# Twelve of the gathered value rows added before the second expert stage, in one streaming-encoder step

## What is computed

```python
e = (jnp.take_along_axis(i1, j // PEER_TOPK, axis=-1) * N_KEYS
     + jnp.take_along_axis(i2, j % PEER_TOPK, axis=-1))
gate = jax.nn.softmax(top_s, axis=-1).astype(xt.dtype)
u = jnp.take(u_experts, e, axis=0)
v = jnp.take(v_experts, e, axis=0)
act = jax.nn.gelu(jnp.einsum('td,thkd->thk', xt, u), approximate=False)
return jnp.einsum('thk,thkd->td', gate * act, v)
```

## Time and profile before

| | |
|---|---|
| timed runs | 1658.46 us median, 1656.03 to 1667.42, 3 runs |
| profiled execution | 1659.93 us, of which its span 1657.1 |
| mean granted TensorE clock | 0.969 of full speed |
| busy, share of the span | TensorE 93%, VectorE 77%, GpSimd 50%, ScalarE 39% |
| DMA, mean over the span | 246 GB/s |

### The profile page before, as it was taken

One profiled execution on the slowest core, in us unless ns is written; L12 is line 12 of the kernel. 1 busy time (PEld: TensorE's weight loads), 2 busy tenths in 40 slices (PEclk: granted clock), 3 DMA queues, 4 the chain that ended last, 5 costly groups with the idle time before them and its releaser, 6 DMA issues.

```text
span 1657.1 us, 26947 instructions
## 1 busy us (share of the span) xinstructions
PE 1540.6 (93%) x9360; PEld 1505.7 (91%) x9360; DVE 1281.3 (77%) x2590; ACT 649.2 (39%) x838; POOL 831.5 (50%) x497
## 2 busy tenths in 40 slices
PE   6995188999999998999999998999999999999996
PEld 6995088999899998999999998999999999999996
DVE  7999998468899998678777741377777777777775
ACT  5332053333333333566665642433333333333332
POOL 5797043333666765666666676234444443344301
PEclk9998589999999999999999999999999999999998
DMA  4221021222766776799999999588998999999851
GB/s 172 90 76 51 0 80 39 90 76 86 245 224 224 267 246 217 284 361 368 359 359 361 348 386 392 184 313 328 344 341 328 356 336 327 329 343 342 327 187 54
DMA packets 149502, 407.59 MB, mean 246 GB/s; under 512 B 12224, under 2 KB 75968, under 8 KB 147648
## 3 DMA queue, kind: packets, MB, share of 16 engines
q1 hardware_dynamic: 89776, 215.27, 38.0%
q0 software_dynamic: 36864, 134.23, 21.6%
q10 hardware_dynamic: 22800, 57.42, 8.9%
HBM read 349.99 MB, written 56.89 MB: 246 GB/s over the span
## 4 chain that ended last, share of the span: by engine, by line
PE 74%; DMA 5%; DVE 1%; ACT 1%; POOL 0%; issue 0%; DVEq 0%; ACTq 0%
PE ps_unit L752 30%; PE ps_unit L812 18%; PE ps_misc L812 17%; PE ps_unit L568 5%; DMA acts_dram<-act_ring 3%; PE ps_misc L786 2%; DMA raw<-stream 1%; PE ps_misc L712 1%; ACT gates L1063 1%; DMA rows<-u_rows,expert 0%; DVE y_all L1623 0%; POOL w_lo L447 0%; ACT act_ring L1035 0%; PE ps_unit L699 0%; DVE gate L1448 0%
## 5 line engine op out<-in xcount | busy, mean ns | idle before, releaser
L447 POOL TENSOR_TENSOR w_lo<-raw,w_hi 128x1024 fp32r<-128x1024 f32 x172 | 423.9, 2469 | 349.2 <-ACT w_hi L867 238.6
L752 PE MATMUL ps_unit<-mov_hi,w_hi 128*128 128x416 f32 x1024 | 366.0, 357 | 8.5 <-POOL w_lo L447 8.5
L532 POOL DMA_INDIRECT rows<-v_rows,expert x128 | 207.1, 1618 | 318.4 <-DVE sums L1357 309.5
L752 PE MATMUL ps_unit<-mov_hi,w_lo 128*128 128x416 f32 x1024 | 362.8, 354 | 0.0
L752 PE MATMUL ps_unit<-mov_lo,w_hi 128*128 128x416 f32 x1024 | 359.7, 351 | 0.0
L867 ACT ACTIVATE w_hi<-raw 128x1024 fp32r<-128x1024 f32 x300 | 315.7, 1053 | 86.4 <-ACT act_ring L1035 60.4
L1087 ACT ACTIVATE prod_hi<-prod 128x416 fp32r<-128x416 f32 x128 | 70.7, 552 | 368.7 <-PE ps_misc L812 367.4
L1543 DVE TENSOR_TENSOR prod_lo<-prod,prod_hi 128x416 fp32r<-128x416 f32 x128 | 75.7, 592 | 171.2 <-ACT prod_hi L1087 171.1
L752 PEld LDWEIGHTS ps_unit<-mov_hi,w_hi 128*128 128x128 f32 x1024 | 193.8, 189 | 10.8 <-ACT w_hi L867 5.3
L752 PEld LDWEIGHTS ps_unit<-mov_lo,w_hi 128*128 128x128 f32 x1024 | 194.2, 190 | 2.8
L752 PEld LDWEIGHTS ps_unit<-mov_hi,w_lo 128*128 128x128 f32 x1024 | 193.5, 189 | 1.5
(11 more groups left out here) (214 smaller groups left out, 2820.0 us busy)
## 6 DMA issues: line engine op xcount, KB each, us to landing
raw<-stream SPq DMA_DIRECT2D x300, 512.0 KB, 4.7
acts_dram<-act_ring ACTq DMA_DIRECT2D x128, 208.0 KB, 5.5
gates_dram<-gates ACTq DMA_DIRECT2D x13, 2048.0 KB, 10.6
gates_in<-gates_dram SPq DMA_DIRECT2D x16, 1664.0 KB, 14.5
acts_in<-acts_dram SPq DMA_DIRECT2D x32, 832.0 KB, 7.3
hid<-x_t SPq DMA_DIRECT2D x4, 544.0 KB, 6.9
rows<-u_rows,expert POOLq DMA_INDIRECT x128, 6.8
rows<-v_rows,expert POOLq DMA_INDIRECT x128, 7.7
```

Source lines behind the costliest of these rows:

```text
L447: nc.gpsimd.tensor_tensor(w_lo[:, j, :], raw[:, j, :], w_hi[:, j, :].bitcast(F32), ALU.subtract).then_inc(lo_made, 1)
L532: nc.gpsimd.indirect_dma_start(out=rows[:, n % ROWS_RING, :], out_offset=None, in_=table, in_offset=bass.IndirectOffsetOnAxis(ap=expert[:, ...
L752: last = nc.tensor.matmul(dense_psum(j), w[:, j, k * P:(k + 1) * P], m[:, k, 0:DENSE], start=(k == 0 and n == 0), stop=(k == KC - 1 and n ...
```

## The change

The first twelve row additions move from the second expert stage to the point right after the last dot product on VectorE, in front of `product(0)`; `weight`, which they need, moves with them. The GELU of the gathered tokens' dots moves on ScalarE to unit 164 (lap 30 of the first stage), between that unit's split and its read-out. `sums_until(v)` starts from 12 and spreads the other 116 over the same blocks, v = 3 to 119. `fetched_by(u)` lets GpSimd issue up to twelve more fetches from unit 167 on: one after the split of unit 167, two after 168, one after 169, two after 170, one after 171, and the rest behind them as buffers come free. Arithmetic and its order are the same.

```diff
+EARLY_SUMS = 12
+GELU_LAP = U_BEFORE + GTS + 3
 def sums_until(v):
-    return SLOTS * (min(max(v + 1, FIRST_SUM), LAST_SUM) - FIRST_SUM) // (LAST_SUM - FIRST_SUM)
+    n = min(max(v + 1, FIRST_SUM), LAST_SUM) - FIRST_SUM
+    return EARLY_SUMS + (SLOTS - EARLY_SUMS) * n // (LAST_SUM - FIRST_SUM)
 def fetched_by(u):
-    return min(min(heads, DOTS_EARLY) + groups, SLOTS) + ROWS_RING
+    sums = 3 * max(u - FIRST_U - RING * GELU_LAP - 2, 0) // 2
+    return min(min(heads, DOTS_EARLY) + groups, SLOTS) + ROWS_RING + min(sums, EARLY_SUMS)
...
+            def gelu_of_dots():
+                act.wait_ge(row_used, SLOTS)
+                nc.scalar.activation(gelu[:], dots[:], ACT.Gelu).then_inc(gelu_made, 1)
             for lap in range(N_U // RING - U_AFTER, N_U // RING):
                 for j in range(RING):
-                    u_unit(lap, j)
+                    u_unit(lap, j, between=gelu_of_dots if (lap, j) == (GELU_LAP, 0) else None)
...
-                if v == 0:
-                    act.wait_ge(row_used, SLOTS)
-                    nc.scalar.activation(gelu[:], dots[:], ACT.Gelu).then_inc(gelu_made, 1)
...
             dots_to(SLOTS)
+            dve.wait_ge(gelu_made, 1)
+            dve.wait_ge(gate_made, 2)
+            nc.vector.tensor_tensor(weight[:], gelu[:], gate[:, DTILES * HEADS:].rearrange("p h k -> p (h k)"),
+                                    ALU.mult).then_inc(weight_made, 1)
+            dve.wait_ge(weight_made, 1)
+            for s in range(EARLY_SUMS):
+                add_row(s)
             for v in range(AHEAD):
                 product(v)
...
-            summed = 0
+            summed = EARLY_SUMS
...
-                if v == FIRST_SUM - 1:
-                    dve.wait_ge(gelu_made, 1)
-                    dve.wait_ge(gate_made, 2)
-                    nc.vector.tensor_tensor(weight[:], gelu[:],
-                                            gate[:, DTILES * HEADS:].rearrange("p h k -> p (h k)"),
-                                            ALU.mult).then_inc(weight_made, 1)
-                    dve.wait_ge(weight_made, 1)
```

## The result

The changed kernel is slower by a little: over 20 timed runs of each kernel its median is 1665.72 us against 1660.50, and the ratio is 1.0027, with a 95% interval from 1.0015 to 1.0038. That is 4.5 us of 1660.5, between 2.5 and 6.3. The measured median lies inside the range given and within 1% of no change, but the change of 4.5 us is more than five times the 0.8 us forecast, and the interval leaves out both the forecast and the case of no effect. One of the 20 runs of the kernel before took 6023.74 us; it counts in the median, which it shifts by 0.35 us, and not in the ratio. The profiled execution took 1666.71 us, 1664.2 of them span, 6.8 more than the one before.

What follows compares the result with a forecast made beforehand. TensorE, busy 93% of the span, was taken to bound the kernel. Terms of 0 plus a TensorE stop of 0.5 us before unit 171, about 0.8 with unit 165's meeting, gave 1658.46 + 0.8 = 1659.3 us; range 1654 to 1667.

Steps and rivals of the forecast that it cites:

- the price of 0 for the second stage: Second expert stage: taking twelve additions and twelve gathers out gains 0, since TensorE waits for neither.
- The bound of 1.7 us on a gain: Second expert stage: a gain is at most TensorE's waits from 1062 on, 0.7 + 1.0 = 1.7 us.
- GELU hidden: ScalarE after unit 164's split: the GELU fits idle time from 1025.46, cost 0; `weight` ready at about 1026.
- stands behind `add_row(11)`: VectorE's queue: `product(0)` waits for the twelfth addition, ready at 1053.6; ScalarE stopped 4.0 us, TensorE 0.5 before unit 171.
- Landing of 7.0 us: Twelfth addition's gather, issued after unit 169's split at 1044.7: lands 7.0 us later, at 1051.7.
- One or two fit: GpSimd's gaps of 2.13 to 2.53 us before splits: room for one or two gather issues of 0.95 to 1.68.
- Who stands behind the new wait: `product(0)` delays `product_high(0)` on ScalarE, then unit 171's split, then TensorE: 0.5 us stop, about 0.8 in all.
- the slower one: Rival, chance 0.14: the twelfth row, landing in 9.7 us, holds VectorE's queue; costs 6.1 us, 1664.6.
- Hidden: Rival, chance 0.27: the twelfth addition's fetch lands within 6.5 us, so no effect; 1658.5.
- faster: Rival, chance 0.07: fewer gathers and additions spare the second stage waits, bounded by 1.7 us; 1656.8.
- The rule on the port: VectorE with two SBUF inputs and GpSimd reading SBUF exclude each other; a split loses up to 1.28 us.
- The landing of 3.2 us: Skill's estimate for a 512 KB gather: the wait ends 3 us early and the change costs 0.

Runs made afterwards that it cites:

- e1: Changed kernel, with the first two products on VectorE put ahead of `weight` and the twelve additions; ratio to the kernel before 0.9999 (0.9985 to 1.0013).
- e2: Changed kernel, with ScalarE's three `product_high` moved behind later splits, VectorE's queue kept; ratio to the kernel before 1.0015 (1.0002 to 1.0027).
- e3: Changed kernel, with the running sum of the twelve early additions held in PSUM; ratio to the kernel before 0.9998 (0.9981 to 1.0014).
- e4: Changed kernel with eight early additions instead of twelve, gathers still moved forward; ratio to the kernel before 1.0002 (0.9988 to 1.0016).
- e5: Changed kernel with eight early additions and no gathers moved forward; ratio to the kernel before 1.0009 (0.9992 to 1.0027).

## Why the prediction was right about the range and wrong about the way

The measured time lies inside the range, but that says little. The range, 1654 to 1667, is wide against the change: it reaches 6.5 us to either side of the 1660.50 of the kernel before, and it was drawn from the scatter of three runs. The forecast of 0.8 us was too small by a factor of more than five, and both steps that set it, VectorE's queue and the twelfth gather, were off in the same direction.

- **What bounds the kernel, and the price of 0 for the second stage:** right. From 1100 to 1600 TensorE runs 2656 matmuls in both traces, though VectorE is busy for 378.4 us there instead of 391.2. The bound of 1.7 us on a gain was built wrongly: its 0.7 and 1.0 are two engines' waits at the same hand-over, and the row ends at 1600; behind that, TensorE waits 1.3 and 0.5 us more, before and after alike.
- **GELU hidden:** its 0.3 us are, its place isn't. I read ScalarE as idle from 1025.46, but the GELU stands behind a wait for the spill of an earlier unit, 1.4 us here. It ran 1.5 us before the read-out of unit 164, where I had it 5.1 before; in e1 it was 3.9, behind a spill wait of 2.2, so the rest hangs on how long TensorE's stop before unit 164 was in that execution. (The rounding that stands ahead of the GELU on ScalarE is that of unit 166, not of unit 164.) And `weight`, put at next to nothing, took 3.48 us beside a split. Together they made the additions start 2.35 us after that read-out instead of 4.3 ahead of it.
- **The failing step: `product(0)` "stands behind `add_row(11)`", whose row lands at 1051.7 and comes last, the first eight additions being "over at about 1043".** The length of the eight was right: 17.0 us, from 1033.92 to 1050.89, three of them stretched. But they started 6.6 us late against the read-out, and the last four, which I had waiting for their rows, waited for none and took 7.4 us, one beside a split. ScalarE's wait was 8.4 us instead of 4.0. Measured from the read-out of unit 164, `product(0)` was ready 27.35 us behind it instead of 23.05. By an estimate from the landing above, about half of these 4.3 us comes from the twelfth row, which landed 2.2 us late on that count, and the other half is the 2.2 us by which VectorE's queue ended behind it. I had seen the exclusion in the convolutions and priced it for three additions and for GpSimd's splits; I didn't sum it through to the end of either queue.
- **How much the late start counts:** no run varies it alone. In e2 the additions began 0.78 us behind the read-out of unit 164 instead of 2.35, and `product(0)` began 27.3 us behind it, against 26.7 in the changed kernel: five additions were stretched there, not four, as the split of unit 171 came among them. Less that fifth stretch, about 2 us, it would have begun some 1.4 us sooner than in the changed kernel, which is an estimate of what the start is worth.
- **Landing of 7.0 us:** measured 6.1 to 6.4. It was shorter than summed, but the gather went out later and the queue ended later still. In e3, without the stretching, the landing did come last, and ScalarE waited 3.6 us where I had forecast 4.0.
- **"One or two fit" between the splits:** two gathers beside additions took 1.76 + 0.30 + 1.07 us, more than the gap of 2.13, and shifted the split of 169. e4 against e5 puts the gathers' whole effect on ScalarE's wait at about 1 us.
- **Who stands behind the new wait:** right, link by link: `product(0)`, `product_high(0)`, the split of 171, TensorE. The last link's slack was about right too: by the rows of before, the split of 171 was over at 1051.25 + 2.42 = 1053.67 and TensorE began the unit at 1062.20 - 4.53 = 1057.67, 4.0 us later, of which 3.9 are left when the usual 0.14 us between a split and TensorE's start is taken off; waits of 3.6 (e3) and 2.7 (e4) stopped nothing, 8.4 stopped 4.1.
- **The rivals:** the slower one, at 0.14, had the right place and, with 6.1 us, the size of the 6.06 measured; its cause, a landing of 9.7 us, wasn't the one at work, so the near agreement is luck, in its size. Hidden and faster are ruled out for this kernel by the trace and the ratio.
- **The rule on the port:** the Trainium skill's page "SBUF — State Buffer" (section "Who interferes with whom") says that such instructions exclude each other. The trace agrees: 3.23 against 1.28 us for an addition beside a split, and 1.29 at most in e3, where the running sum lay in PSUM. I had weighed the rule for the loss of GpSimd only. The landing of 3.2 us that I had estimated from the Trainium skill's "DMA: Bandwidth & Descriptors" (section "Anatomy of one DMA — SWDGE (gpsimd) path") isn't borne out: the gathers from 1036 to 1060 took 6.1 and more.

Of the 6.06 us local loss the whole shows 4.5 (2.5 to 6.3). In the profiled execution after the change, the stop before unit 164 happened to be 3.0 us without a fall of the clock. Over the traces of the kernel before, the changed one and e1 to e5 that stop ranges from 3.0 to 5.6 us, so a single pair of executions doesn't show the change's price; the yardstick and the 20 runs do.

## What to carry to other kernels

Idle time on an engine is room only for work that stands behind everything the other engines wait for; put the urgent short instructions (here two of half a microsecond) first, and the filler after them. When filler moves beside another engine's work, reprice its own duration there, not just the harm it does, and follow the sum through each in-order queue to the engine that sets the end. And look for what can be moved out of a full stretch of transfers before moving more work into the stretch behind it: here holding eight early gathers back was worth 0.35% (0.21 to 0.49).

## What the hardware showed that I had not expected

A tiny instruction can be held as long as a big one: the 128 x 128 multiplication, 0.285 us when nothing is beside it, took 3.34 to 3.75 us in the runs that put it beside GpSimd's splits. That is longer than one split of 2.4 us: in the changed kernel and in e1 to e5 it began during one split, wasn't let in before the next, and ended about 0.15 us behind the end of that one (in e3: begun at 1030.30, the splits over at 1031.41 and 1033.75, ended at 1033.91). The stretched additions of the changed kernel each met a single split with no other directly behind it. With the running sum in PSUM the additions took 1.28 us again, the splits 2.40, the gather issues 0.95 instead of 1.76.

TensorE's fall to the lower of its two clocks (1.2 GHz, a granted clock of 0.50) after a stop wasn't the same each time, and neither was its price. After the 4.1 us stop before unit 171 the granted clock was 0.50 from 1064 to 1066, and the unit took 6.20 instead of 4.53 us. In e3 a stop of 3.4 us before unit 164 was followed by 0.50 from 1026 to 1032, and units 164 to 171 took 39.00 us together, 2.8 more than eight times 4.53. After the stop of 3.0 us before unit 164 in the changed kernel, the granted clock stayed at 1.00.
